# Attention heads in pairs: both heads' logit products next to each other, one output bank and one scaling per pair

## The chip, the cores and the metric

The kernel runs on one core of one Trainium2 chip. The metric is the device time of one execution in microseconds (us), as the median of several runs.

## What is computed

Two transformer blocks in sequence on 256 tokens with 2048 features, all float32. The part that the change touches is the attention of the first block: 16 "forgetting" heads (kind f, causal, with a decay added to the logits) and 16 "dilated" heads (kind d, three dilated windows merged by counting how often each key is seen), each 64 wide:

```python
proj = rms_norm(h, gain) @ w_in                       # fq fk fv fg dq dk dv
# f: p = softmax(q k^T / 8 + (c_q - c_k), causal);  o = p v
# d: q, k with rotary positions; three windows (128,1) (512,4) (2048,16);
#    o = sum over windows of softmax(lse) * softmax(q k^T / 8 in the window) v
mixed = concat(rms_norm(fox_o), rms_norm(dil_o))      # 2 x 1024 columns
h = h + mixed @ w_out
h = h + peer(rms_norm(h))                             # 16384 experts, top 16 of 8 heads
```

The second block (convolution, recurrence, gates) comes behind it and is not touched.

## The kernel before

**Weights.** All large products take their weights in units of 128x1024 floats, 512 KB each. For each unit u, SyncE loads `raw` (ring of 4), ScalarE rounds it to `whi` (`split`, line 1360), VectorE makes the rest `wlo` (`split`, line 760), and TensorE adds three products, high x high, high x low and low x high, in a PSUM bank (`group_f`, `group_t`). ScalarE and VectorE prepare unit u+3 in their step u. So ScalarE's `split(u + 3)` waits for TensorE to end unit u, and TensorE needs its result three units later.

**Units and ticks.** TensorE calls `tick(u)` behind unit u, and VectorE and ScalarE have a `step(u)` for it. Units 57 to 64 are the last dilated key projection (`dk` 1; 12 products of 512 columns per unit), units 65 to 96 are the forgetting heads' query and key projections `fq`/`fk` 0 to 7, two units each with 24 products of 256 columns per unit. The table `HEAD_START` (lines 109 to 112) hangs the 32 heads on these units, and `head_steps` spreads each over its phases:

- A: TensorE makes the logits, 64 rows deep (a head's q and k lie on rows 0 to 63 or 64 to 127 of `dqT`, `dkT`, `fqT`, `fkT`): query half 0 by 128 keys, query half 1 by 256 keys (lines 480, 481). VectorE adds the mask (for an f head made on the spot in `MB`, lines 812, 813) and takes the row's extreme (line 819), ScalarE makes the exponentials in `EB`.
- B, of d heads alone: VectorE multiplies by the counts and sums (line 824), and takes the reciprocal.
- C: TensorE turns the three 128x128 blocks round (line 490), ScalarE copies them to `PB` (line 1407).
- D: TensorE multiplies `PB` with `VV` (line 500), VectorE scales the two 64-wide results from the bank to `TM` (line 837).

A d head takes four ticks, an f head three (A, C, D). Before, heads start one per tick. An f head starts when its `fq`/`fk` pair has been copied out of its bank. f heads 14 and 15 start at ticks 97 and 98, behind the last unit, where no projection stands beside them (lines 683 to 686); the norm of `TM` and then the output projection wait for them.

The queues run in program order. The order within a tick is that of the heads' start. Small results share banks 4 to 7 in turn (`plan.side`), and whoever fills one waits until its last content is gone (`vacant`). `EB`, `PB` and `dn` have six slots.

Of the kernel before, what the change touches and what calls it, by code (L numbers as in the profile page):

```python
# [80 lines left out]
class Plan:  # L81
# [21 lines left out]
    def group(self, name, i, key, j, banks):  # L103
# [5 lines left out]
HEAD_START = [("d", h, 57 + h) for h in range(8)]  # L109
HEAD_START += [("d", 8, 67), ("d", 9, 68), ("f", 0, 69), ("f", 1, 70), ("d", 10, 71), ("d", 11, 72), ("f", 2, 73), ("f", 3, 74),  # L110
               ("d", 12, 75), ("d", 13, 76), ("f", 4, 77), ("f", 5, 78), ("d", 14, 79), ("d", 15, 80), ("f", 6, 81), ("f", 7, 82)]
HEAD_START += [("f", 2 * i + s, 69 + 4 * i + s) for i in range(4, 8) for s in range(2)]
HEAD_TICKS = range(57, 102)
TURN_AFTER = {("dq", 1): 0, ("fq", 0): 1}


def head_steps():

    at = {t: [] for t in HEAD_TICKS}
    for q, (kind, h, t) in enumerate(HEAD_START):  # L120
        for n, phase in enumerate("ABCD" if kind == "d" else "ACD"):
            at[t + n].append((q, kind, h, phase))
    return at
# [8 lines left out]
def _build(nc, I, out, ctx):  # L132
# [147 lines left out]
    HEADS = head_steps()  # L280
    hfill = {}
    for t in HEAD_TICKS:
        if t == 67:
            turns.append([plan.side() for _ in range(4)])
        for q, kind, h, phase in HEADS[t]:
            if phase != "B":
                hfill[q, phase] = plan.side()
# [161 lines left out]
    def _(e):  # L449
# [17 lines left out]
        def head(q, kind, h, phase):  # L467
            hp = slice(64 * (h % 2), 64 * (h % 2) + 64)
            ft, i = h // 2, q % 6
            vb = (0 if kind == "f" else 1024) + h * 64  # L470
            if phase == "A":
                qs, ks = QK[kind + "qT"], QK[kind + "kT"]
                if kind == "d":
                    for fill in turns[h // 8]:
                        evacuated(fill)
                else:
                    evacuated(G["fq", ft].fills[0])
                    evacuated(G["fk", ft].fills[0])
                b = vacant(hfill[q, "A"])
                mm(b[:, 0:128], qs[hp, ft, 0:128], ks[hp, ft, 0:128], True, True)  # L480
                mm(b[:, 128:384], qs[hp, ft, 128:256], ks[hp, ft, 0:256], True, True).then_inc(s_lg, 1)
            if phase == "C":
                if kind == "d":
                    w.wait_ge(s_cn, 2 * sum(k == "d" for k, _, _ in HEAD_START[:q + 1]))
                else:
                    w.wait_ge(s_ex, 2 * q + 2)
                w.wait_ge(s_const, 32)
                b = vacant(hfill[q, "C"])
                for j in range(3):
                    tr = turn_round(b[:, j * 128:j * 128 + 128], EB[:, i, j * 128:j * 128 + 128])  # L490
                tr.then_inc(s_ht, 1)
            if phase == "D":
                evacuated(hfill[q, "C"])
# [3 lines left out]
                b = vacant(hfill[q, "D"])  # L497
                for t in range(2):
                    for kt in range(t + 1):
                        ov = mm(b[:, 64 * t:64 * t + 64], PB[:, i, (t + kt) * 128:(t + kt) * 128 + 128],  # L500
                                VV[:, kt, vb:vb + 64], kt == 0, kt == t)
                ov.then_inc(s_ov, 1)
# [93 lines left out]
        def tick(u):  # L596
            if u in HEAD_TICKS and u < G["fk", 7].end:
                for q, kind, h, phase in HEADS[u]:
                    if phase != "B":
                        head(q, kind, h, phase)  # L600
# [82 lines left out]
        for u in range(G["fk", 7].end, HEAD_TICKS.stop):  # L683
            for q, kind, h, phase in HEADS[u]:
                if phase != "B":
                    head(q, kind, h, phase)
# [59 lines left out]
    def _(e):  # L746
# [50 lines left out]
        def head(q, kind, h, phase):  # L797
            i = q % 6
            vb = (0 if kind == "f" else 1024) + h * 64
            E, d = EB[:, i, :], dn[:, i, :]  # L800
            cs = [slice(0, 128), slice(128, 384)]
            nf = sum(k == "f" for k, _, _ in HEAD_START[:q])
            nd = q - nf
            if phase == "A":
                if q >= 6:
                    w.wait_ge(s_ht, q - 5)
                    evacuated(hfill[q - 6, "D"])
                w.wait_ge(s_att, 32)
                M = MB[:, nf % 4, :]
                if kind == "f":  # L810
                    w.wait_ge(s_cb, 16)
                    tt(M[:, 0:128], mskF[:, 128:256], CB[:, h, 0:128], ALU.subtract).then_inc(s_mask, 1)
                    tt(M[:, 128:384], mskF, CB[:, h, :], ALU.subtract).then_inc(s_mask, 1)
                    w.wait_ge(s_mask, 2 * nf + 2)
                b, n = hfill[q, "A"]
                w.wait_ge(s_lg, q + 1)
                for t in range(2):
                    m_ = M[:, cs[t]] if kind == "f" else mskD if t else mskF[:, 128:256]
                    e.tensor_tensor_reduce(E[:, cs[t]], banks[b][:, cs[t]], m_, -1.0, 3.0e38,  # L819
                                           ALU.add, ALU.min, d[:, t:t + 1]).then_inc(s_free[b] if t else s_mx, 1)  # L820
            if phase == "B":
                w.wait_ge(s_ex, 2 * q + 2)
                for t in range(2):
                    e.tensor_tensor_reduce(E[:, cs[t]], E[:, cs[t]], cnt1 if t else cnt0, 1.0, 0.0,
                                           ALU.mult, ALU.add, d[:, 2 + t:3 + t]).then_inc(s_cn, 1)
                w.wait_ge(s_cn, 2 * nd + 2)
                e.reciprocal(d[:, 4:6], d[:, 2:4]).then_inc(s_rd, 1)
            if phase == "C" and kind == "f":
                w.wait_ge(s_ex, 2 * q + 2)
                e.reciprocal(d[:, 4:6], d[:, 2:4]).then_inc(s_rd, 1)  # L830
            if phase == "D":
                b, n = hfill[q, "D"]
                w.wait_ge(s_ov, q + 1)
                w.wait_ge(s_rd, q + 1)
                w.wait_ge(s_turn, 4 if q < 8 else 8)
                for t in range(2):
                    o = e.tensor_scalar(TM[:, t, vb:vb + 64], banks[b][:, 64 * t:64 * t + 64], d[:, 4 + t:5 + t], None, ALU.mult)
                o.then_inc(s_free[b], 1)
# [222 lines left out]
        def step(u):  # L1061
            if u in HEAD_TICKS and u < G["fk", 7].end:
                for q, kind, h, phase in HEADS[u]:
                    head(q, kind, h, phase)
# [77 lines left out]
        for u in range(G["fk", 7].end, HEAD_TICKS.stop):  # L1142
            for q, kind, h, phase in HEADS[u]:
                head(q, kind, h, phase)

        for fill in hfill.values():
            evacuated(fill)
        w.wait_ge(s_ov, 32)
# [193 lines left out]
    def _(e):  # L1342
# [46 lines left out]
        def head(q, kind, h, phase):  # L1389
            i = q % 6  # L1390
            E, d = EB[:, i, :], dn[:, i, :]
            cs = [slice(0, 128), slice(128, 384)]
            if phase == "A":
                w.wait_ge(s_mx, q + 1)
                evacuated(hfill[q, "A"])
                for t in range(2):
                    if kind == "f":
                        act(E[:, cs[t]], E[:, cs[t]], ACT.Exp, bias=d[:, t:t + 1], scale=-1.0,
                            accum_out=d[:, 2 + t:3 + t]).then_inc(s_ex, 1)
                    else:  # L1400
                        act(E[:, cs[t]], E[:, cs[t]], ACT.Exp, bias=d[:, t:t + 1], scale=-1.0).then_inc(s_ex, 1)
            if phase == "C":
                b, n = hfill[q, "C"]
                if q >= 6:
                    w.wait_ge(s_ov, q - 5)
                w.wait_ge(s_ht, q + 1)
                act(PB[:, i, :], banks[b][:, 0:384], ACT.Copy).then_inc(s_free[b], 1)
# [72 lines left out]
        def step(u):  # L1480
            if u in HEAD_TICKS and u < G["fk", 7].end:
                for q, kind, h, phase in HEADS[u]:
                    head(q, kind, h, phase)
# [61 lines left out]
        for u in range(G["fk", 7].end, HEAD_TICKS.stop):  # L1545
            for q, kind, h, phase in HEADS[u]:
                head(q, kind, h, phase)
        warm()

        for fill in hfill.values():  # L1550
            evacuated(fill)
        w.wait_ge(s_ov, 32)
# [203 lines left out]
```

## Time and profile before

| what | value |
|---|---|
| median of 3 runs | 3015.35 us (3012.07 to 3016.42) |
| the profiled execution's own time | 3016.64 us |
| its span, first to last instruction | 3014.9 us |
| TensorE matmul busy | 2931.1 us, 97% of the span |
| VectorE, ScalarE busy | 1816.1 us (60%), 1349.6 us (45%) |
| mean granted TensorE clock | 0.986 of full |
| the heads' stretch, tick 57 to the last head's scaling | from 185.56 us to 376.69 us |

PE is TensorE's matmuls, PEld its weight loads, DVE is VectorE, ACT ScalarE. A float32 product is made in two passes, each with a weight load: one head's phase A is 4 loads and 4 matmuls in the trace, phase D is 6, phase C is 3. A matmul's duration in a row runs until its result is out, and matmuls overlap; how fast they follow each other is read from their starts.

### The profile page before, as it was taken

How to read it: one execution, taken by the hardware profiler on the slowest of the kernel's cores; microseconds unless marked ns; L12 is line 12 of the kernel's file. 1: busy time of each engine (PE TensorE's matmuls, PEld its weight loads, DVE VectorE, ACT ScalarE, POOL GpSimd, SP SyncE). 2: the span in 40 equal slices, each digit the busy share in tenths (PEclk: the TensorE clock that was granted, in tenths of full speed). 3: DMA queues.
4: the chain of work that ended last, by engine and by line, in shares of the span. 5: the costliest groups of instructions: out<-in, count | busy, mean ns of one | idle time of the engine just before them, and what ended most of it. 6: DMA issues, size and time to landing. Idle time of an engine off the chain costs nothing. (4 is left out here: it accounts for less than half of the span.)

```text
span 3014.9 us, 47881 instructions
## 1 busy us (share of the span) xinstructions
PE 2931.1 (97%) x19478; PEld 2698.1 (89%) x19478; DVE 1816.1 (60%) x3033; ACT 1349.6 (45%) x1809; POOL 0.2 (0%) x4
## 2 busy tenths in 40 slices
PE   8999999999999999999999999997999999999988
PEld 6878878999999999998888888886989999999876
DVE  5556555477888874444555555556577765555555
ACT  4444444344444444444444444444554544444444
POOL 0000000000000000000000000000000000000000
PEclk9999999999999999999999999998999999999999
DMA  6643346455556665556666677764554455555554
GB/s 211 209 136 109 123 148 201 151 184 183 183 182 210 210 216 183 182 186 195 222 221 222 205 232 237 235 210 159 160 183 147 147 164 188 184 183 182 187 166 157
DMA packets 180091, 557.33 MB, mean 185 GB/s; under 512 B 20624, under 2 KB 51616, under 8 KB 176928
## 3 DMA queue, kind: packets, MB, share of 16 engines
q1 hardware_dynamic: 177568, 537.49, 55.0%
q10 hardware_dynamic: 2304, 16.78, 1.4%
q8 instruction: 155, 2.54, 0.3%
q14 instruction: 64, 0.52, 0.1%
HBM read 533.21 MB, written 20.99 MB: 184 GB/s over the span
## 5 line engine op out<-in xcount | busy, mean ns | idle before, releaser
L760 DVE TENSOR_TENSOR wlo<-raw,whi 128x1024 fp32r<-128x1024 f32 (+1 forms) x965 | 1180.0, 1224 | 1051.4 <-ACT whi L1352 1048.2
L1352 ACT ACTIVATE whi<-raw 128x1024 fp32r<-128x1024 f32 (+1 forms) x965 | 1017.2, 1056 | 1055.4 <-PE bank L453 1040.6
L453 PE MATMUL bank<-aH,whi 128*128 128x256 f32 (+1 forms) x3984 | 1138.7, 286 | 0.0
L453 PE MATMUL bank<-aH,wlo 128*128 128x256 f32 (+1 forms) x3984 | 1128.3, 283 | 2.0 <-DVE wlo L760 2.0
L453 PE MATMUL bank<-aL,whi 128*128 128x256 f32 (+1 forms) x3984 | 1127.1, 283 | 0.0
L453 PE MATMUL bank<-whi,aH 128*128 128x512 f32 x2624 | 859.2, 391 | 5.2 <-DVE aH L763 3.8
L453 PEld LDWEIGHTS bank<-aH,whi 128*128 128x128 f32 (+1 forms) x3984 | 762.9, 191 | 8.2 <-issue 7.6
L453 PEld LDWEIGHTS bank<-aH,wlo 128*128 128x128 f32 (+1 forms) x3984 | 762.0, 191 | 3.2 <-DVE wlo L760 2.6
L453 PEld LDWEIGHTS bank<-aL,whi 128*128 128x128 f32 (+1 forms) x3984 | 762.5, 191 | 0.5
L453 PE MATMUL bank<-wlo,aH 128*128 128x512 f32 x1600 | 625.1, 391 | 0.8 <-DVE wlo L760 0.8
L453 PEld LDWEIGHTS bank<-whi,aH 128*128 128x128 f32 x2624 | 494.6, 188 | 111.3 <-DVE aH L763 4.0
L453 PEld LDWEIGHTS bank<-wlo,aH 128*128 128x128 f32 x1600 | 301.7, 189 | 64.3 <-DVE wlo L760 2.0
L453 PE MATMUL bank<-whi,aL 128*128 128x512 f32 x576 | 225.2, 391 | 0.0
L1352 ACT ACTIVATE aH<-HB 128x256 fp32r<-128x256 f32 x128 | 53.5, 418 | 214.2 <-DVE HB L763 214.2
L1352 ACT ACTIVATE HB<-bank 128x256 f32<-128x256 f32 (+1 forms) x192 | 85.0, 443 | 123.7 <-PE bank L453 123.7
L453 PEld LDWEIGHTS bank<-whi,aL 128*128 128x128 f32 x576 | 108.7, 189 | 22.5
L763 DVE TENSOR_TENSOR aH<-HB,aH 128x256 fp32r<-128x256 f32 x128 | 54.3, 425 | 61.9 <-ACT aH L1352 61.9
L894 DVE TENSOR_SCALAR HB<-small,HB 128x128 f32<-128x128 f32 x256 | 87.4, 341 | 0.0
L453 PE MATMUL bank<-HB 128*128 128x128 f32 x576 | 77.6, 282 | 3.1 <-DVE HB L1174 3.1
L453 PEld LDWEIGHTS bank<-HB 128*128 128x128 f32 x576 | 72.6, 198 | 3.3 <-issue 3.3
L893 DVE TENSOR_SCALAR HB<-small,HB 128x128 f32<-128x128 f32 x256 | 71.8, 280 | 0.0
L1352 ACT ACTIVATE EB<-EB,dn 128x128 f32<-128x128 f32 x64 | 27.2, 448 | 76.6 <-DVE dn L819 76.5
(183 smaller groups left out, 1653.8 us busy)
## 6 DMA issues: line engine op xcount, KB each, us to landing
raw<-in_w_down SPq DMA_DIRECT2D x256, 512.0 KB, 3.6
raw<-in_w_up SPq DMA_DIRECT2D x256, 512.0 KB, 3.8
raw<-in_w_in SPq DMA_DIRECT2D x176, 512.0 KB, 3.6
raw<-in_w_out SPq DMA_DIRECT2D x32, 512.0 KB, 3.8
raw<-in_w_pq SPq DMA_DIRECT2D x32, 512.0 KB, 4.2
gate_scratch<-HB ACTq DMA_DIRECT2D x16, 1024.0 KB, 4.9
raw<-in_w_o SPq DMA_DIRECT2D x32, 512.0 KB, 4.2
raw<-in_w_pg SPq DMA_DIRECT2D x32, 512.0 KB, 4.1
```

The source lines that it names most:

```text
L453: return e.matmul(o, lhsT, rhs, start=start, stop=stop, skip_group_check=True)
L760: e.tensor_tensor(wlo[:, s, 0:n], raw[:, r, 0:n], whi[:, s, 0:n].bitcast(F32), ALU.subtract).then_inc(s_lo, 1)
L763: return e.tensor_tensor(o, a, b, op)
L893: e.tensor_scalar(AB[:, i, 0, c, :], iota, JT[:, 0, t:t + 1], None, ALU.is_equal).then_inc(s_oh, 1)
L894: e.tensor_scalar(AB[:, i, 1, c, :], iota, JT[:, 1, t:t + 1], JT[:, 2, t:t + 1], ALU.is_equal, ALU.mult).then_inc(s_oh, 1)
L1352: return e.activation(o, i, f, **k)
```

## The change

The heads are taken in pairs (2i, 2i+1). `PAIRS` starts 16 pairs where 32 heads started: d pairs at ticks 57, 59, 61, 63, 67, 71, 75, 79 and f pairs at 69, 73, 77, 81, 85, 89, 93, 97. In phase A the two heads' products alternate, head 2i on rows 0 to 63 and head 2i+1 on rows 64 to 127, into two banks. C has two banks, D writes both heads into one bank, and one VectorE operation scales 128x256 values to `TM`. The reciprocals of a pair are one operation. The ring of six slots now holds three pairs.

```diff
-HEAD_START = [("d", h, 57 + h) for h in range(8)]
...
+PAIRS = [("d", 0, 57), ("d", 1, 59), ("d", 2, 61), ("d", 3, 63), ("d", 4, 67), ("f", 0, 69), ("d", 5, 71), ("f", 1, 73),
+         ("d", 6, 75), ("f", 2, 77), ("d", 7, 79), ("f", 3, 81), ("f", 4, 85), ("f", 5, 89), ("f", 6, 93), ("f", 7, 97)]
...
-            if phase != "B":
-                hfill[q, phase] = plan.side()
+            if phase in "AC":
+                hfill[q, phase] = [plan.side(), plan.side()]
+            if phase == "D":
+                hfill[q, phase] = [plan.side()]
... TensorE
-                b = vacant(hfill[q, "A"])
-                mm(b[:, 0:128], qs[hp, ft, 0:128], ks[hp, ft, 0:128], True, True)
-                mm(b[:, 128:384], qs[hp, ft, 128:256], ks[hp, ft, 0:256], True, True).then_inc(s_lg, 1)
+                b = [vacant(fill) for fill in hfill[q, "A"]]
+                for t in range(2):
+                    for x in range(2):
+                        hp = slice(64 * x, 64 * x + 64)
+                        lg = mm(b[x][:, 128 * t:128 + 256 * t], qs[hp, pair, 128 * t:128 * t + 128], ks[hp, pair, 0:128 * t + 128], True, True)
+                        if t:
+                            lg.then_inc(s_lg, 1)
...
+                    w.wait_ge(s_ex, 4 * q + 4)
...
+                for fill in hfill[q, "C"]:
+                    evacuated(fill)
...
+                for t in range(2):
+                    for x in range(2):
+                        for kt in range(t + 1):
+                            ov = mm(b[:, 128 * t + 64 * x:128 * t + 64 * x + 64],
+                                    PB[:, 2 * (q % 3) + x, (t + kt) * 128:(t + kt) * 128 + 128],
+                                    VV[:, kt, vb + 64 * x:vb + 64 * x + 64], kt == 0, kt == t)
... VectorE
+                for x in range(2):
...
+                        w.wait_ge(s_mask, 4 * nf + 2 * x + 2)
+                    b, n = hfill[q, "A"][x]
+                    w.wait_ge(s_lg, 2 * q + x + 1)
...
-                for t in range(2):
-                    o = e.tensor_scalar(TM[:, t, vb:vb + 64], banks[b][:, 64 * t:64 * t + 64], d[:, 4 + t:5 + t], None, ALU.mult)
-                o.then_inc(s_free[b], 1)
+                tt(TM[:, :, vb:vb + 128].rearrange("p t (x c) -> p t x c", x=2),
+                   banks[b][:, 0:256].rearrange("p (t x c) -> p t x c", t=2, x=2),
+                   d2[:, :, 4:6].rearrange("p x t -> p t x").unsqueeze(3).to_broadcast([128, 2, 2, 64]), ALU.mult).then_inc(s_free[b], 1)
```

**TensorE between two units of the `dk` projection.** Before, every tick from 60 to 64 holds one head's D, the next one's C and a third one's A (`VV,PB` is D, `small,EB` is C, `dkT,dqT` is A; the first and the last row are the projection):

```order
L453 MATMUL bank<-whi,aL 128x512
L453 MATMUL bank<-VV,PB 128x64 x3
L465 MATMUL bank<-small,EB 128x128 x3
L453 MATMUL bank<-dkT,dqT 128x128
L453 MATMUL bank<-dkT,dqT 128x256
L453 MATMUL bank<-whi,aH 128x512
```

With the change an odd tick holds C of one pair and A of the next:

```order
L452 MATMUL bank<-whi,aL 128x512
L464 MATMUL bank<-small,EB 128x128 x6
L452 MATMUL bank<-dkT,dqT 128x128 x2
L452 MATMUL bank<-dkT,dqT 128x256 x2
L452 MATMUL bank<-whi,aH 128x512
```

The even ticks hold D alone, `VV,PB 128x64 x6`. The two heads' A products now stand together, once every second unit.

**TensorE behind the last unit.** Before (two single heads, 14 and 15, one D of head 13 ahead of them; the last row is the norm's transposes):

```order
L453 MATMUL bank<-aH,wlo 128x256
L453 MATMUL bank<-VV,PB 128x64 x3
L453 MATMUL bank<-fkT,fqT 128x128
L453 MATMUL bank<-fkT,fqT 128x256
L465 MATMUL bank<-small,EB 128x128 x3
L453 MATMUL bank<-fkT,fqT 128x128
L453 MATMUL bank<-fkT,fqT 128x256
L453 MATMUL bank<-VV,PB 128x64 x3
L465 MATMUL bank<-small,EB 128x128 x3
L453 MATMUL bank<-VV,PB 128x64 x3
L465 MATMUL bank<-small,VV 128x128 x32
```

With the change (one pair):

```order
L452 MATMUL bank<-aH,wlo 128x256
L452 MATMUL bank<-fkT,fqT 128x128 x2
L452 MATMUL bank<-fkT,fqT 128x256 x2
L464 MATMUL bank<-small,EB 128x128 x6
L452 MATMUL bank<-VV,PB 128x64 x6
L464 MATMUL bank<-small,VV 128x128 x32
```

The two heads go through A, C and D together, in three steps where there were four, and no D stands ahead of them.

**VectorE behind the last unit, with the change** (the second head's masks, its two sums with the logits, then the pair's reciprocal and scaling, and the norm's first square):

```order
L768 TENSOR_TENSOR MB<-attc,CB 128x128
L768 TENSOR_TENSOR MB<-attc,CB 128x256
L825 ISA EB,dn<-bank,MB 128x128
L825 ISA dn 128x1
L825 ISA EB,dn<-bank,MB 128x256
L825 ISA dn 128x1
L838 RECIPROCAL dn<-dn 128x2x2
L768 TENSOR_TENSOR TM<-bank,dn 128x2x128
L771 ISA VV,st<-TM 128x512
```

The second head's masks stand behind the first head's logits on VectorE; before they stood behind the whole of the first head's A.

## Rows read from the trace of the kernel before

**Rows 1.** The page, part 1: busy time, share of the span, instructions
```profile
PE 2931.1 (97%) x19478; PEld 2698.1 (89%) x19478; DVE 1816.1 (60%) x3033; ACT 1349.6 (45%) x1809; POOL 0.2 (0%) x4
```

**Rows 2.** Busy time by stretch: f units, bare tail; PEclk, DMA share, GB/s last
```profile
235.00:365.00 130.00, 128.23 (x989) 117.48 (x987) 72.99 (x246) 62.78 (x139) 0.00 (x0) 1.00 0.36 116
365.00:378.00 13.00, 7.28 (x26) 5.15 (x26) 4.79 (x20) 5.84 (x17) 0.00 (x0) 0.56 0.24 81
```

**Rows 3.** Timeline, PE alone, ticks 91 to 94: start us, duration us, group
```profile
345.22 0.36 PE L453 MATMUL bank<-aH,whi 128*128 128x256 f32 x1
...
348.77 0.36 PE L453 MATMUL bank<-aH,whi 128*128 128x256 f32 x1
...
352.67 0.38 PE L453 MATMUL bank<-aH,whi 128*128 128x256 f32 x1
...
355.64 0.49 PE L465 MATMUL bank<-small,EB 128*128 128x128 f32 x3
356.06 0.92 PE L453 MATMUL bank<-fkT,fqT 64*128 64x128 f32 x4
356.91 0.39 PE L453 MATMUL bank<-aH,whi 128*128 128x256 f32 x1
357.13 0.28 PE L453 MATMUL bank<-aL,whi 128*128 128x256 f32 x1
357.25 0.28 PE L453 MATMUL bank<-aH,wlo 128*128 128x256 f32 x1
```

**Rows 4.** The same A stretch, timeline cut at its third and fourth pass
```profile
356.39 0.59 PE L453 MATMUL bank<-fkT,fqT 64*128 64x256 f32 x2
...
356.61 0.38 PE L453 MATMUL bank<-fkT,fqT 64*128 64x256 f32 x1
```

**Rows 5.** Timeline, tick 69: PE's C and A, ACT's work ahead
```profile
243.29 0.49 PE L465 MATMUL bank<-small,EB 128*128 128x128 f32 x3
244.07 0.89 PE L453 MATMUL bank<-fkT,fqT 64*128 64x128 f32 x4 [0.28 <-issue]
...
242.66 1.04 ACT L1352 ACTIVATE whi<-raw 128x1024 fp32r<-128x1024 f32 x1
243.61 0.36 ACT L1352 ACTIVATE fkT<-bank 128x256 f32<-128x256 f32 x1
```

**Rows 6.** Timeline, PE at tick 66: D, C, second half of the turning
```profile
227.94 0.78 PE L453 MATMUL bank<-VV,PB 128*128 128x64 f32 x6
...
229.27 0.55 PE L465 MATMUL bank<-small,EB 128*128 128x128 f32 x3 [0.55 <-DVE dn L824]
...
231.09 1.06 PE L465 MATMUL bank<-small,TM 128*128 128x128 f32 x8 [0.40 <-DVE TM L837]
```

**Rows 7.** Timeline, DVE and ACT around tick 68: wlo, B of a d head, exponentials
```profile
239.25 1.23 DVE L760 TENSOR_TENSOR wlo<-raw,whi 128x1024 fp32r<-128x1024 f32 x1 [1.95 <-ACT whi L1352]
240.39 0.28 DVE L824 CUSTOM_DVE_ANT_0 EB<-EB,attc 128x128 f32<-128x128 f32 x1
...
241.06 0.17 DVE L827 RECIPROCAL dn<-dn 128x2 f32<-128x2 f32 x1
...
241.95 0.80 ACT L1352 ACTIVATE EB<-EB,dn 128x128 f32<-128x128 f32 x2 [2.80 <-DVE dn L819]
```

**Rows 8.** Timeline of all engines behind the last unit, heads 14 and 15
```profile
365.40 0.89 PE L453 MATMUL bank<-fkT,fqT 64*128 64x128 f32 x4 [0.91 <-issue]
366.27 0.62 DVE L763 TENSOR_TENSOR MB<-attc,CB 128x128 f32<-128x128 f32 x2
366.92 0.29 DVE L819 CUSTOM_DVE_ANT_0 EB<-bank,MB 128x128 f32<-128x128 f32 x1
...
368.46 0.18 ACT L1352 ACTIVATION_READ_ACCUMULATOR EB<-EB,dn 128x1 f32 x1
...
368.70 0.90 PE L465 MATMUL bank<-small,EB 128*128 128x128 f32 x3 [2.42 <-ACT EB L1352]
...
369.70 0.49 ACT L1352 ACTIVATE PB<-bank 128x384 f32<-128x384 f32 x1 [1.05 <-PE bank L465]
...
374.64 1.54 PE L453 MATMUL bank<-VV,PB 128*128 128x64 f32 x6 [0.64 <-ACT PB L1352]
376.22 0.47 DVE L837 TENSOR_SCALAR TM<-bank,dn 128x64 f32<-128x64 f32 x2 [2.97 <-PE bank L453]
```

More of the change, by code:

```diff
@@ L465, in turn_round, with heads @@
             return e.transpose(o, src, ident)
[L467 to L470, printed above, removed]
+        def heads(q, kind, pair, phase):
             if phase == "A":
@@ L597, in tick @@
             if u in HEAD_TICKS and u < G["fk", 7].end:
-                for q, kind, h, phase in HEADS[u]:
+                for q, kind, pair, phase in HEADS[u]:
                     if phase != "B":
-                        head(q, kind, h, phase)
+                        heads(q, kind, pair, phase)
             if DOWN0 <= u < DOWN0 + ROUTE:
@@ L683, in _ @@
         for u in range(G["fk", 7].end, HEAD_TICKS.stop):
-            for q, kind, h, phase in HEADS[u]:
+            for q, kind, pair, phase in HEADS[u]:
                 if phase != "B":
-                    head(q, kind, h, phase)
+                    heads(q, kind, pair, phase)
         norm_turn(1, VV)
@@ L795, in tails, with heads @@
                     hook(kp)
[L797 to L800, printed above, removed]
+        def heads(q, kind, pair, phase):
+            vb = (0 if kind == "f" else 1024) + pair * 128
+            e0 = 2 * (q % 3)
+            d2 = dn[:, e0:e0 + 2, :]
             cs = [slice(0, 128), slice(128, 384)]
-            nf = sum(k == "f" for k, _, _ in HEAD_START[:q])
+            nf = sum(k == "f" for k, _, _ in PAIRS[:q])
@@ L1062, in step @@
             if u in HEAD_TICKS and u < G["fk", 7].end:
-                for q, kind, h, phase in HEADS[u]:
-                    head(q, kind, h, phase)
+                for q, kind, pair, phase in HEADS[u]:
+                    heads(q, kind, pair, phase)
             if u == G["dq", 0].first + 1:
@@ L1142, in _ @@
         for u in range(G["fk", 7].end, HEAD_TICKS.stop):
-            for q, kind, h, phase in HEADS[u]:
-                head(q, kind, h, phase)
-        for fill in hfill.values():
+            for q, kind, pair, phase in HEADS[u]:
+                heads(q, kind, pair, phase)
+        for fill in [x for y in hfill.values() for x in y]:
             evacuated(fill)
-        w.wait_ge(s_ov, 32)
+        w.wait_ge(s_ov, 16)
         for c in range(1, 8, 2):
@@ L1481, in step @@
             if u in HEAD_TICKS and u < G["fk", 7].end:
-                for q, kind, h, phase in HEADS[u]:
-                    head(q, kind, h, phase)
+                for q, kind, pair, phase in HEADS[u]:
+                    heads(q, kind, pair, phase)
             if DOWN0 <= u < DOWN0 + ROUTE:
```

134 lines of the change are left out of this document (63 added, 71 removed).

## The prediction

> **What bounds the kernel now.** I read the page first: TensorE's matmuls are busy for 97% of the span, VectorE 60%, ScalarE 45% [rows 1]. Then the busy time by stretch, for the place that the change touches: among the `fq`/`fk` units TensorE is busy for 128.2 of 130 us at full clock while VectorE works 73.0 us and ScalarE 62.8 us, and the DMA share is 0.36; behind the last unit TensorE works 7.3 of 13 us at a mean granted clock of 0.56 [rows 2]. So there are two kinds of place. Among the units only time on TensorE's own queue counts, its waits included. Behind the last unit it is a chain through all three engines. The timeline then prices both, and 0.2% of the kernel, 6 us, is about what a measurement can tell from no change.
>
> **Pace of TensorE.** Projection products of 256 columns follow each other every 0.12 us (357.13 to 357.25), so a bare unit of 24 takes 2.88 us [rows 3]. From one unit's first product to the next one's it is 3.55 us with a D between (345.22 to 348.77), 3.90 us with an A (348.77 to 352.67), 4.24 us with a C and an A (352.67 to 356.91) [rows 3]. So D costs 0.67, A 1.02 and C 0.34 us. What is in A? Its 256-column pass takes 0.22 us (356.39 to 356.61) [rows 4], a 128-column pass half of it, so its four passes are 0.66 us. The other 0.36 us belong to the change of form, from 128-row products to 64-row ones and back. Half of it is seen at the way out: the last pass is followed after 0.30 us, not 0.22 (356.61 to 356.91), and the first projection product after 0.22, not 0.12 (356.91 to 357.13) [rows 3, 4]. The other half is at the way in.
>
> **The change, part by part.**
>
> *Logit products side by side.* The same passes, in half as many stretches. Of 32 stretches 30 stood among units, and 15 stand there now, so 15 ways in and out go: 15 x 0.36 = 5.4 us. What the two halves of the rows do to each other no row shows, since no two A stretches touch before. Bounds: at worst each of the three steps from one half to the other inside a pair costs what the change of form costs, 3 x 0.36 = 1.08 us, 16.2 us over 15 pairs (that is a rival below). At best passes of different halves overlap. The order is head 0 twice, head 1 twice, for 128 columns and then for 256; with starts in that order the second pass of one head can cover the first of the other, and a pair's 1.32 us would shrink by 0.43, which is 6.4 us over 15. But each pass needs a weight load of 128 columns, and if loads come one after the other at the 0.11 us of the short passes, the short ones cannot overlap at all and only one 0.22 us pass is covered: 0.2 us per pair, 3.1 us. I take half of that smaller gain, 1.6 us, because the rows nearest to it, the single stretches, show passes strictly one after the other.
>
> The Trainium skill ("TensorEngine Tiling (Array Packing)", Key Properties) says that changing the tiling mode drains TensorE and changing only the tile does not, so by it the steps inside a pair would be free; no row here shows that half of the rule.
>
> *The new ticks.* C and D have the passes they had. A pair's D is 12 passes in one stretch; what its ends cost is within hundredths of a us, taken as nothing.
>
> *Waits of TensorE that go.* At tick 69 A starts 0.78 us behind C's start, where 0.42 is the normal step (355.64 to 356.06) [rows 3, 5]. ScalarE copies `fkT` out until 243.97, and that copy is late because the exponentials of the head of tick 68 and a split of 1.04 us stand ahead of it [rows 5]. This recurs at ticks 73, 77 and 81. With the change ticks 68, 72, 76 and 80 have no A, and the copy is done within some 1.5 us of the unit's end, a whole unit before it is needed: 4 x 0.35 = 1.4 us. At tick 66 C starts 1.33 us behind D, 0.7 more than D's 6 passes take, waiting for a B that VectorE runs behind the rotary work; then the turning waits 0.40 us for the scaling of a head [rows 6]. With the change the last B of the `dk` part is in tick 64, ahead of the rotary work, and the scaling finds VectorE free: 1.1 us.
>
> *One D that loses its cover.* Behind the last unit TensorE waits 0.91 us for the copy of `fkT` before A [rows 8], and head 13's D lies ahead of that wait, hidden. With the change the D of f pair 6 is in tick 95 and nothing stands there: 0.6 us given back.
>
> *VectorE.* The scaling is 1 operation for a pair where 4 stood, and a reciprocal goes. It works 73 of 130 us there [rows 2], so among units this is worth nothing. New on it: a pair's A holds the masks and sums of two heads in a row, and ScalarE's two sets of exponentials come ahead of the split for the unit three further on. That delays `whi` by 0.7 to 0.9 us where two whole units lie in between. No load is moved, and the ring of four raw buffers is ahead at a DMA share of 0.36.
>
> *New lateness, C against the softmax.* Count from the end of A's stretch on TensorE. An f pair: first sums done at 0.4 (they start when that head's own passes are done, ahead of the other's last two), second masks 0.62, second sums 0.65 and the exponentials 1.07 behind them (sums from 366.92, exponentials to 368.64 [rows 8]), so 2.8 us. The next C comes after a unit, 2.97 us, in the last four f pairs, and after a unit and a D in the others. It is met by 0.1 us. A d pair: two sums end at 1.1, two exponentials of 0.8, split 1.04, `wlo` 1.23, then B of both heads at 0.67 each [rows 7] end near 5.6; C comes after two units, 5.8 us. Met by 0.2 us. I cost both at nothing.
>
> *Behind the last unit.* Before, the scaling ends at 376.69 [rows 8]. With the pair, counting on the same clock: first sums at 366.92 as before (VectorE sets that, not TensorE), second sums end 0.65 + 0.62 + 0.65 later at 368.84, exponentials at 369.91, C 369.97, its second half 0.65 later (three passes at half clock), `PB` of the second head from 371.62 to 372.11, D with 12 passes where 6 took 1.58 us from 374.64 to 376.22, so 1.58 + 6 x 0.22 = 2.9 us, and one scaling of 0.42 us: 375.5. That is 1.2 us earlier. The norm and the output projection follow as they did.
>
> **Sum.** 5.4 + 1.6 + 1.4 + 1.1 - 0.6 + 1.2 = 10.1 us less than the profiled execution's 3016.6. That execution is 1.3 us above the median of the runs, so I forecast 3015.35 - 10.1, about **3005 us**. The granted clock adds noise that no term carries: the bare tail runs at half clock in stretches that end where they end, and starting the next work 9 us earlier against them can win or lose 2 us.
>
> **The rivals.**
>
> 1. *Full overlap of the halves.* The loads too would run side by side, and the gain on top of 8.5 us is 6.4 instead of 1.6: 15 us, 3000.4 us. For it: the halves share no row and no bank. Against it: every pass in the rows of a stretch waits for its load. The Trainium skill ("TensorE: Matmul & The Clock Gate", Part 3) says that matmuls in different row groups start some 4 ns apart, and that loads overlap matmuls of another group; taken alone for this order that is this rival, and no row here shows it. Chance 0.14.
>
> 2. *The step between halves costs as much as the change of form* (the other side). The pair's three inner steps, 1.08 us, are more than the 0.36 it saves, so 15 x 0.72 = 10.8 us are lost on TensorE, another 2 us behind the last unit, where the clock is half; against it stand the 3.1 us of waits and tail, and the time is 3015.35 + 9.7 = 3025 us. It decides from 0.6 us per pair of inner steps on. For it: the change of form is dear, and nothing shows that it is not the step of rows that is paid. Against it: no wait is needed between halves that share nothing. Chance 0.07.
>
> 3. *The softmax of a pair misses C.* The margins above are 0.1 and 0.2 us. If every one of 15 pairs made TensorE wait 0.4 us, 6 us come back, and 4 us remain: 3011 us, within 0.2%. For it: all latencies grow by one head's work. Against it: 4 of the f pairs have a D ahead of C, which gives 1.2 us more. Chance 0.17.
>
> 4. *Given back later*: the earlier finish meets an unlucky run of half-clock stretches, here and in the later stages. Then 3 to 5 us stay: 3011 us. Chance 0.07.
>
> **How the numbers follow.** The forecast (8 to 13 us gained) has 0.55. Faster by over 0.2% takes the forecast, rival 1 and a part of rivals 3 and 4: 0.77. Within 0.2%: the rest of those two, 0.15. Slower: rival 2 and a little for what I don't see, 0.08. The range leaves out rival 2 and the tails of the others: it reaches from full overlap, 3000 us, to rivals 3 and 4, 3012 us.
>
> **What the profile after would show.** 16 A stretches of 8 passes. If I am right, an A tick of one pair costs 1.5 to 1.7 us over the bare unit, not 2.04; if rival 1 is, below 1.3; if rival 2 is, above 2.4. C follows A at ticks 69, 73, 77, 81 in 0.34 us per head, and `fkT` is no longer what A waits for. Rival 3 shows as PE idle ahead of `small,EB`, released by ScalarE's `EB` or VectorE's `dn`. Tick 66 has no gap. Behind the last unit it should be 10.1 us from A's start to the scaling's end, not 11.3. Wrong above all would be a stretch elsewhere that changes, since nothing behind the first block's heads is touched.

## The result and the profile after

| what | before | with the change |
|---|---|---|
| median | 3015.35 us (5 runs) | 2998.84 us (5 runs, 2992.67 to 2999.56) |
| ratio | | 0.9943, 95% interval 0.9929 to 0.9958 |
| span of the profiled execution | 3014.9 us | 2990.9 us |

It is 16.5 us faster by the medians, 0.57% (0.42 to 0.71%) by the ratio. The direction is as forecast, the size is not: 10.1 us were predicted, and 2998.8 lies 1.2 us under the range.

The page after, part 1, to be held against [rows 1]:

```profile
PE 2908.7 (97%) x19478; PEld 2684.3 (90%) x19478; DVE 1806.9 (60%) x2969; ACT 1348.0 (45%) x1809; POOL 0.2 (0%) x4
```

TensorE has the same 19478 matmuls and is busy for 22.4 us less, so time was saved while it works, not only in its waits (a part of it is the granted clock, see below). Busy time by stretch, first the ticks 69 to 94, then the bare tail, as in [rows 2]:

```profile
235.00:345.00 110.00, 109.78 (x920) 104.14 (x919) 62.94 (x191) 57.41 (x130) 0.00 (x0) 1.00 0.41 130
347.50:359.00 11.50, 5.26 (x26) 4.33 (x26) 4.19 (x15) 5.76 (x14) 0.00 (x0) 0.63 0.26 85
```

Among the units nothing but TensorE is short: it is busy for all but 0.2 of 110 us. The table cuts both traces at the same five points of the program. The times are differences of starts in the trace.

| from ... to ... | before | after | gain |
|---|---|---|---|
| first A ... first C | 10.60 us | 8.01 us | 2.6 |
| first C ... last product of unit 96 | 167.43 | 153.05 | 14.4 |
| that product ... last scaling to `TM` | 13.11 | 11.75 | 1.4 |
| last scaling ... output projection's first product | 11.42 | 10.81 | 0.6 |
| together | 202.56 | 183.62 | 18.9 |

The 14.4 us are the step to explain. Timeline of an A stretch of a pair, PE alone, the same place in a unit as [rows 3]:

```profile
305.38 0.28 PE L452 MATMUL bank<-aL,whi 128*128 128x256 f32 x1
305.50 0.28 PE L452 MATMUL bank<-aH,wlo 128*128 128x256 f32 x1
305.71 0.93 PE L452 MATMUL bank<-fkT,fqT 64*128 64x128 f32 x8
306.57 0.38 PE L452 MATMUL bank<-aH,whi 128*128 128x256 f32 x1
306.79 0.28 PE L452 MATMUL bank<-aL,whi 128*128 128x256 f32 x1
```

The eight passes of a pair take 0.86 us until the next projection product (305.71 to 306.57). The four passes of one head took 0.85 (356.06 to 356.91 [rows 3]). Two heads cost what one did. Cut the same timeline at 305.80 us and the view shows how:

```profile
305.71 0.38 PE L452 MATMUL bank<-fkT,fqT 64*128 64x128 f32 x2
```

Two passes have started, and together they last 0.38 us, hardly more than one. The trace's own starts of the eight are 305.713 and 305.720, then 305.927 and 305.933, 306.038 and 306.045, 306.257 and 306.264: the halves of the rows run as a pair of passes 7 ns apart, weight loads included.

The price of a pair is 1.07 us from the last product before it to the first one behind it, and 0.10 for the slower step after that (306.57 to 306.79, where 0.12 is normal), less the 0.12 of a normal step: 1.05 us. Two single heads cost 2.04 by the prediction's count, and 2.08 when they are counted at the same places as the pair. The period of the f pairs decides between the two: from A at tick 89 to A at tick 93 before takes 15.53 us (336.29 to 351.82) and after 14.82 (320.55 to 335.37), of which 0.29 are a new wait of C (below), so a pair saves 1.00 us, and 2.04 is the better count. Between the first C and the last unit's end lie 28 single A before and 14 pairs after, so 28 x 1.02 - 14 x 1.05 = 13.9 us. The waits that went give 2.5 us, the D without cover takes 0.6 and new waits of C 1.4: 14.4, which is the whole of that stretch.

The waits are gone as forecast. Timeline of PE at ticks 66 and 69, to be held against [rows 6] and [rows 5]:

```profile
223.47 1.45 PE L452 MATMUL bank<-VV,PB 128*128 128x64 f32 x12
224.75 1.92 PE L464 MATMUL bank<-small,TM 128*128 128x128 f32 x16
...
236.24 0.87 PE L464 MATMUL bank<-small,EB 128*128 128x128 f32 x6
237.04 0.93 PE L452 MATMUL bank<-fkT,fqT 64*128 64x128 f32 x8
```

At tick 66 the turning follows 1.28 us behind the start of D's twelve passes. At tick 69 A starts 0.80 us behind C, which is now six passes. No row has a bracket for a wait.

Two small waits are new, and the PE view does not mark them either, because they hide in the overlap of pipelined matmuls. PE at tick 90, and what ScalarE does there:

```profile
309.42 0.28 PE L452 MATMUL bank<-aH,wlo 128*128 128x256 f32 x1
309.78 0.87 PE L464 MATMUL bank<-small,EB 128*128 128x128 f32 x6
310.41 0.36 PE L452 MATMUL bank<-aH,whi 128*128 128x256 f32 x1
...
309.14 0.49 ACT L1360 ACTIVATE EB<-EB,dn 128x256 f32<-128x256 f32 x1
309.54 0.19 ACT L1360 ACTIVATION_READ_ACCUMULATOR EB<-EB,dn 128x1 f32 x1
```

C starts 0.36 us behind the last product, where 0.12 is normal, and right behind the second head's last exponential (309.54 + 0.19 = 309.73). With the step behind it that is 0.29 us, at ticks 86, 90 and 94; four d pairs lose 0.12 each.

Behind the last unit, all engines, to be held against [rows 8]:

```profile
348.46 0.36 ACT L1360 ACTIVATE fkT<-bank 128x256 f32<-128x256 f32 x1
...
348.92 0.93 PE L452 MATMUL bank<-fkT,fqT 64*128 64x128 f32 x8 [1.52 <-issue]
...
353.44 1.54 PE L464 MATMUL bank<-small,EB 128*128 128x128 f32 x6 [3.59 <-ACT EB L1360]
354.44 1.07 ACT L1360 ACTIVATE PB<-bank 128x384 f32<-128x384 f32 x2 [1.05 <-PE bank L464]
...
355.61 2.79 PE L452 MATMUL bank<-VV,PB 128*128 128x64 f32 x12 [0.63 <-ACT PB L1360]
358.44 0.42 DVE L768 TENSOR_TENSOR TM<-bank,dn 128x256 f32<-128x256 f32 x1 [4.84 <-PE bank L452]
```

From A's start to the scaling's end it is 9.95 us (348.92 to 358.87). The chain is one of waits: C waits for both heads' exponentials, D for both copies, the scaling for all twelve passes.

**The granted clock.** The profiled executions differ by 24 us, the medians by 16.5. Behind the output projection's first product no instruction was changed, and yet that rest took 2626.7 us before and 2621.2 after. TensorE's clock was at 1.2 GHz (granted clock 0.5) for 47.8 us of it before and for 34.1 us after, not counting what lies behind TensorE's last matmul. In nine of the eleven profiled executions of this study the rest less half of its half-clock time lies between 2602.8 and 2604.3 us; the other two have 2604.8 (e7_table_tail) and 2601.7 (e8_table_again). So the half-clock time, which runs from 34.1 to 47.8 us, is worth up to 6.8 us from one execution to the next, and what it leaves unexplained up to 3 us. One such place, 193.4 us behind that first product, by stretch, in the profile after and in a second execution of the same program (columns as in [rows 2]):

```profile
563.10:569.90 6.80, 6.11 (x55) 6.14 (x55) 4.37 (x8) 0.00 (x0) 0.00 (x0) 1.00 0.31 96
```

```profile
562.80:569.60 6.80, 5.56 (x26) 5.59 (x27) 2.34 (x5) 0.00 (x0) 0.00 (x0) 0.50 0.37 125
```

Same program, same work, 55 matmuls in 6.8 us in one and 26 in the other. Ahead of it TensorE was idle for most of the time in both, busy for 0.72 of 3.1 us and for 0.88 of 2.8 us. So below I compare the stretch from the first A to the output projection's first product, which does not depend on the rest, and use the medians as the check. What this comparison does not see is time that an edit adds ahead of the first A (see e9_table_tail_exp).

### The profile page after: what moved, and what is told of

Same layout as the page of the kernel before. It is cut to its first block and busy times, and to the rows that moved or that the text cites. A ratio compares the mean times of both kernels' runs of the same rounds, so it can differ in the third digit from the quotient of the medians.

```text
span 2990.9 us, 47745 instructions
## 1 busy us (share of the span) xinstructions
PE 2908.7 (97%) x19478; PEld 2684.3 (90%) x19478; DVE 1806.9 (60%) x2969; ACT 1348.0 (45%) x1809; POOL 0.2 (0%) x4
## 5 line engine op out<-in xcount | busy, mean ns | idle before, releaser
L452 PEld LDWEIGHTS bank<-whi,aL 128*128 128x128 f32 x576 | 108.5, 188 | 22.4
L768 DVE TENSOR_TENSOR HB<-HB,aL 128x256 f32<-128x256 f32 x126 | 52.8, 419 | 0.0
```

What stands on the lines that cost most here:

```text
L452: return e.matmul(o, lhsT, rhs, start=start, stop=stop, skip_group_check=True)
L768: return e.tensor_tensor(o, a, b, op)
```

## The experiments

The theory after the result is **lockstep** (OVERLAP in the expectations): passes of the two halves run side by side, so a pair costs one head. The rivals: it needs the alternating order; it is the single change of form that pays, not the overlap (MERGE); or the gain is in the joint bank and scaling.

Stretches in us, from the trace of each kernel's profiled execution. "Units" is from the first C to the last product of unit 96, "copy" from there to the last pair's A (before: to head 14's), "tail" from A to the end of the last scaling, "norm" from there to the output projection.

| kernel | first A to C | units | copy | tail | norm | together |
|---|---|---|---|---|---|---|
| before | 10.60 | 167.43 | 1.81 | 11.30 | 11.42 | 202.56 |
| after | 8.01 | 153.05 | 1.80 | 9.95 | 10.81 | 183.62 |
| e1_again | 8.07 | 152.98 | 1.80 | 9.95 | 10.83 | 183.64 |
| e2_same_half | 8.67 | 160.69 | 1.81 | 9.94 | 10.82 | 191.92 |
| e3_head_after_head | 7.89 | 153.10 | 1.80 | 9.94 | 10.99 | 183.72 |
| e4_table_alone | 8.05 | 151.72 | 1.85 | 8.35 | 10.63 | 180.60 |
| e5_turn_per_head | 9.48 | 151.60 | 1.80 | 9.30 | 10.81 | 183.00 |
| e6_output_per_head | 8.03 | 153.06 | 1.85 | 9.35 | 10.63 | 182.92 |
| e7_table_tail | 7.33 | 152.18 | 0.84 | 8.38 | 11.32 | 180.05 |
| e8_table_again | 9.48 | 151.71 | 1.85 | 8.35 | 10.63 | 182.02 |
| e9_table_tail_exp | 6.48 | 151.81 | 0.84 | 8.23 | 10.30 | 177.66 |

### e1_again: the change once more

No edit.

> The changed kernel once more, on the chip of the next three, so that they can be held against it. Theory OVERLAP: the two heads' passes run at the same time on the two halves of the rows, so a pair's phase A (8 passes) takes 0.86 us from its first product to the next projection product, as one head's did. Theory MERGE: the gain is the saved changes of form and waits, the rest was a lucky granted clock. Both expect a ratio to the kernel before of 0.994 to 0.996 here; OVERLAP expects 0.86 us per stretch again, and 183 to 185 us from the first A to the first output projection product (before 202.6).

Measured: 3000.17 us (2994.41 to 3000.52), 3013.45 before on that chip, ratio 0.995 (0.9936 to 0.9963). The stretch repeats to 0.02 us. Its rest has the 47.8 us of half clock that before has, and with those equal the spans differ by 3014.9 - 2997.1 = 17.8 us: that is the change with most of the clock's luck taken out (the first pair still has 1.5 us of it, see below).

### e2_same_half: both heads on rows 0 to 63

```diff
-                        hp = slice(64 * x, 64 * x + 64)
+                        hp = slice(0, 64)
```

> Both heads of a pair read q and k of the even head, rows 0 to 63, so head 2i's logits are made twice and head 2i+1's not at all; passes, banks, order and all other work stay. OVERLAP: the stretch grows by one head's four passes, 0.66 us, to 1.5 us; 15 x 0.66 = 9.9 us among units and some 0.9 us behind them (the first head's logits come while VectorE is still busy, the second's too): 10 us slower than the changed kernel, ratio to before 0.997 to 0.998. MERGE: no difference from the changed kernel.

Measured: 3003.67 us (3002.78 to 3004.81), ratio 0.9967 (0.9955 to 0.9979). Its A stretch, timeline of PE:

```profile
312.35 0.28 PE L452 MATMUL bank<-aH,wlo 128*128 128x256 f32 x1
312.56 1.57 PE L452 MATMUL bank<-fkT,fqT 64*128 64x128 f32 x8
314.07 0.39 PE L452 MATMUL bank<-aH,whi 128*128 128x256 f32 x1
```

The stretch is 1.51 us instead of 0.86, so the overlap is worth 0.65 us per pair. That is the 0.66 us of one head's passes, all of it. Over 15 pairs it is 9.8 us. The units grew by 7.6 us: 14 x 0.65 = 9.1, less the 1.4 us of C's waits, which vanish since a longer A gives the softmax more time. What remains against before, 202.56 - 191.92 = 10.6 us, is what the change gives without overlap, 1.5 us of it by the clock in the first pair (below). The rival that puts all of the gain on the change of form falls. The odd heads' logits are not computed here, so this kernel is of use for its time alone. By the medians it is 3.5 us slower than e1_again, not the 10 that were expected: the stretch is 8.3 us longer (the waits of C went, and the tail did not grow by the expected 0.9), and its profiled execution has 6.8 us less half clock in the rest (41.0 against 47.8), which is worth 3.4. So the 0.65 us per pair are read from the trace, and the medians give only their direction.

### e3_head_after_head: the order of the passes

```diff
-                for t in range(2):
-                    for x in range(2):
+                for x in range(2):
+                    for t in range(2):
```

> The four products of a pair in the order head 0 (128, 256 keys), head 1 (128, 256 keys), not alternating. OVERLAP with starts in program order: only the last pass of head 0 and the first of head 1 can overlap, so the stretch is 1.2 to 1.4 us, 5 to 8 us slower than the changed kernel. OVERLAP with a queue for each half: stretch 0.86 us, time as the changed kernel within 1 us. MERGE: as the changed kernel.

Measured: 2997.79 us (2996.75 to 2999.6), ratio 0.9946 (0.9932 to 0.9959). TensorE is given both products of head 2i and then both of head 2i+1. Its timeline, and the same cut at 305.40 us:

```profile
305.25 0.93 PE L452 MATMUL bank<-fkT,fqT 64*128 64x128 f32 x8
306.11 0.38 PE L452 MATMUL bank<-aH,whi 128*128 128x256 f32 x1
```

```profile
305.25 0.39 PE L452 MATMUL bank<-fkT,fqT 64*128 64x128 f32 x2
```

It still takes 0.86 us, and the two short passes at its start (305.245 and 305.258 in the trace, 13 ns apart) are followed by two more at 305.46. The two wide passes of one head start with the two of the other (305.570 and 305.583). If starts kept the program's order, head 2i would have run its four passes first. The trace does not name the head of a pass; it is read from the columns, two short passes and two wide ones per head. So the order plays no part here: a pass waits for its own half's passes and not for the up to four that were issued ahead of it on the other half.

### e4_table_alone: the kernel before with the new starts

```diff
-HEAD_START = [("d", h, 57 + h) for h in range(8)]
...
+PAIRS = [("d", 0, 57), ("d", 1, 59), ("d", 2, 61), ("d", 3, 63), ("d", 4, 67), ("f", 0, 69), ("d", 5, 71), ("f", 1, 73),
+         ("d", 6, 75), ("f", 2, 77), ("d", 7, 79), ("f", 3, 81), ("f", 4, 85), ("f", 5, 89), ("f", 6, 93), ("f", 7, 97)]
+HEAD_START = [(kind, 2 * pair + x, t) for kind, pair, t in PAIRS for x in range(2)]
```

Everything else stays per head: its own C wait, D bank and scaling.

> The kernel before with only its table of starts changed: heads 2i and 2i+1 start at the same tick, each with its own bank, its own D and two scalings of its own, products head after head. If the place of the heads is all that matters and each half has a queue: within 1 us of the changed kernel (the single scaling is worth 0.5 us behind the last unit). If starts go in program order: 5 to 8 us slower than the changed kernel. MERGE: as the changed kernel.

Measured: 2991.75 us (2990.43 to 2994.84), ratio 0.993 (0.9917 to 0.9944). Since TensorE's queue holds the two heads' A next to each other here too, the table alone brings the whole overlap: the eight passes of a pair take 0.86 us again, read as above from PE's timeline:

```profile
304.95 0.93 PE L452 MATMUL bank<-fkT,fqT 64*128 64x128 f32 x8
305.82 0.38 PE L452 MATMUL bank<-aH,whi 128*128 128x256 f32 x1
```

The stretch is 3.0 us shorter than with the full change, where within 1 us was expected. Its tail, all engines:

```profile
350.62 0.90 PE L464 MATMUL bank<-small,EB 128*128 128x128 f32 x3 [2.33 <-ACT EB L1351]
...
351.84 0.91 PE L464 MATMUL bank<-small,EB 128*128 128x128 f32 x3 [0.31 <-ACT EB L1351]
352.54 2.66 PE L452 MATMUL bank<-VV,PB 128*128 128x64 f32 x12
...
353.96 0.47 DVE L836 TENSOR_SCALAR TM<-bank,dn 128x64 f32<-128x64 f32 x2 [1.98 <-PE bank L452]
...
355.24 0.48 DVE L836 TENSOR_SCALAR TM<-bank,dn 128x64 f32<-128x64 f32 x2 [0.81 <-PE bank L452]
```

The first head's C, D and scaling each run while the second head is one step behind. The joint waits of the change take that overlap away, 8.35 us against 9.95.

### e5_turn_per_head and e6_output_per_head: which joint step costs the 3 us

e5 is the change with one wait for C per head:

```diff
-                if kind == "d":
-                    w.wait_ge(s_cn, 4 * sum(k == "d" for k, _, _ in PAIRS[:q + 1]))
-                else:
-                    w.wait_ge(s_ex, 4 * q + 4)
...
+                    if kind == "d":
+                        w.wait_ge(s_cn, 4 * sum(k == "d" for k, _, _ in PAIRS[:q + 1]) - 2 + 2 * x)
+                    else:
+                        w.wait_ge(s_ex, 4 * q + 2 * x + 2)
```

> The changed kernel, but each head's transposes (phase C) wait for that head's softmax and not for the pair's. Read from the first A to the first output projection product (183.6 us in the changed kernel, 180.6 with the table alone). Theory TURN: the pair's common wait ahead of C is what the changed kernel loses against the table alone: C's late starts of 0.12 us at d pairs and 0.24 us at f pairs go, and behind the last unit the first head's C and copy lie under the second head's exponentials, 0.65 us; 181.5 to 182.5 us in all. Theory OUTPUT: the common D and single scaling is what costs: this run changes nothing, 183.6 us.

e6 is the change with an output bank and a scaling per head:

```diff
-                hfill[q, phase] = [plan.side()]
+                hfill[q, phase] = [plan.side(), plan.side()]
...
+                for x in range(2):
+                    evacuated(hfill[q, "C"][x])
+                    b = vacant(hfill[q, "D"][x])
...
```

> The changed kernel, but phase D with a bank, a semaphore step and two scalings for each head, as before the change; A and C stay paired. TURN: only what lies behind the last unit changes, where the first head's scaling lies under the second's D and the second's D waits alone for its copy: 0.3 to 0.9 us; 182.7 to 183.3 us. OUTPUT: most of the 3 us come back, below 181.5 us. Among units both expect no gain from or loss to the three more operations on VectorE, which waits there anyway.

Measured, one run each: e5 2993.44 us, e6 2994.7 us; the verdict rests on the stretches. In e5 the units lose 1.45 us and the tail 0.65. C of tick 90 again follows after a normal 0.12 us:

```profile
309.90 0.28 PE L452 MATMUL bank<-aH,wlo 128*128 128x256 f32 x1
310.02 0.82 PE L464 MATMUL bank<-small,EB 128*128 128x128 f32 x6
310.60 0.36 PE L452 MATMUL bank<-aH,whi 128*128 128x256 f32 x1
```

Its first A to C is longer (9.48) because that execution spent 6.5 us there at half clock and the one of after 3.4; e4_table_alone and e8_table_again, one program, differ in the same way (8.05 and 9.48). In e6 the units do not move (153.06): one scaling instead of four saves nothing where TensorE is the bound. Tail and norm lose 0.6 and 0.2 us, since D of the first head no longer waits for the second copy: it starts 1.54 us behind C, where 2.17 passed with the change. Together e5 and e6 give 1.45 + 0.65 + 0.6 + 0.2 = 2.9 us, and e4_table_alone gains 3.0. The joint steps are settled for this kernel: they cost 3 us of the stretch and bring nothing.

### e7_table_tail: e4 with the masks a tick early and the last copy ahead of a split

```diff
+    for q, (kind, h, t) in enumerate(HEAD_START):
+        if kind == "f":
+            at[t - 1].append((q, kind, h, "M"))
...
-            split(u + NSPL)
+            if u != G["fk", 7].end - 1:
+                split(u + NSPL)
...
+            if u == G["fk", 7].end:
+                split(u - 1 + NSPL)
```

> The table alone, with the f heads' masks made one tick early on VectorE, and, behind the last unit, ScalarE's copy of fkT and both heads' phase A put ahead of the split for the unit three further on. What should go is the chain behind the last unit: the copy is 1.04 us earlier, and neither the split of 1.22 us nor 0.62 us of masks per head stands between the logits and their sums: 10.2 us from the last projection product to the last scaling should become 8 to 8.7 us. Units as in the table alone, 159.8 us. First A to first output product 178.8 us; ratio to before 0.991 to 0.993.

### e8_table_again: e4 once more, on the same chip

> The table alone once more, beside e7 on the same chip: 180.6 us from the first A to the first output product again, and a ratio to before of 0.992 to 0.994. If its lead over the changed kernel was only clock luck, 0.995. Once the first output projection product has started, every kernel so far took 2603.6 us (2602.9 to 2604.1) plus half of the time at half clock in the profile up to the last stretch; this should hold again.

Measured: e7 2992.9 us (2989.93 to 2994.2), ratio 0.9929 (0.9916 to 0.9943); e8 2993.72 us (2993.44 to 2995.16), ratio 0.9935 (0.9921 to 0.9949). The copy of `fkT` came 1.0 us sooner, but the tail stayed at 8.38. ACT and PE there:

```profile
345.64 0.38 ACT L1360 ACTIVATE fkT<-bank 128x256 f32<-128x256 f32 x1 [3.09 <-PE bank L455]
346.16 0.93 PE L455 MATMUL bank<-fkT,fqT 64*128 64x128 f32 x8 [0.56 <-ACT fkT L1360]
...
349.74 1.04 ACT L1360 ACTIVATE whi<-raw 128x1024 fp32r<-128x1024 f32 x1
350.68 0.84 ACT L1360 ACTIVATE PB<-bank 128x384 f32<-128x384 f32 x2
```

The split that I had moved out of the copy's way stands ahead of the `PB` copies now, 1.04 us of it. No run separates it from the masks; the tail as a whole gained nothing. From the last projection product to the last scaling it is 9.2 us, where 8 to 8.7 were expected. In e8_table_again the stretch is 182.02 us, not the 180.6 expected: 1.43 us more in the first A to C, at 6.5 us of half clock instead of 3.4, and 0.01 elsewhere. Its rest is under the expected 2602.9 to 2604.1 us (2601.7).

### e9_table_tail_exp: that split further back, and the table load ahead

e7 with the split behind tick 98 on both engines, and one small exponential ahead of the heads, so that ScalarE's table is there:

```diff
+        act(st[:, 31:32], cols[:, 0:1], ACT.Exp).then_inc(s_warm, 1)
...
-            if u == G["fk", 7].end:
-                split(u - 1 + NSPL)
+            if u == G["fk", 7].end + 1:
+                split(u - 2 + NSPL)
```

> e7_table_tail with two more edits: the split that was postponed stands behind the last copies to PB (both engines), not ahead of them, and ScalarE makes one exponential of one column ahead of the dk units, so that the 1.28 us load of its table is out of the first pair's chain. Theory (each of the two is a link of a chain that TensorE waits for): from the last pair's A to the last scaling 8.38 in e7_table_tail becomes 7.4 (the 1.04 us split gone from between exponentials and PB), the copy of fkT still starts 0.84 us behind the last projection product; from the first A to the first C 7.3 us or 8.0 become 6.7 or less at full clock; from the first A to the first product of the output projection 178.5 to 179.5 us where e7_table_tail took 180.05, ratio to the kernel before 0.992. Rival (what ends these stretches is TensorE's own half clock and not the engines' chain): both stretches stay within 0.3 us of e7_table_tail, ratio 0.993. The rest of the kernel, behind the output projection's first product, stays at 2603 to 2605 us plus half of its half-clock time.

Measured: 2993.9 us (2993.15 to 2995.49), ratio 0.9936 (0.9923 to 0.995). The stretch is the shortest of all, 177.66 us, 6.0 under the change. The first A to C is 6.48 us, 0.85 less than in e7_table_tail, neither with any half clock: the table load was a link of the first pair's chain, as this kernel expected. In e3_head_after_head, where TensorE was never at half clock there, the load and the wait read:

```profile
187.30 1.28 ACT L1360 ACT_TABLE_LOAD   x1 [6.67 <-DVE dn L825]
...
193.54 0.88 PE L464 MATMUL bank<-small,EB 128*128 128x128 f32 x6 [1.29 <-DVE dn L832]
```

But the load was moved and not saved. It now stands ahead of three splits, and TensorE waits for `wlo` (ACT, then PE):

```profile
118.02 1.28 ACT L1360 ACT_TABLE_LOAD   x1
119.31 0.21 ACT L1360 ACTIVATE st<-cols 128x1 f32<-128x1 f32 x1
119.42 2.98 ACT L1360 ACTIVATE whi<-raw 128x1024 fp32r<-128x1024 f32 x3
...
121.85 0.50 PE L455 MATMUL bank<-wlo,aH 128*128 128x512 f32 x1 [0.37 <-DVE wlo L762]
...
136.32 0.50 PE L455 MATMUL bank<-wlo,aH 128*128 128x512 f32 x1 [0.58 <-DVE wlo L762]
```

The first A starts at 187.06 us, where every other kernel has it between 185.56 and 186.05 and e7_table_tail at 185.81. That is 1.25 us lost ahead of the stretch for 0.85 gained in it.

The tail missed its 7.4: it took 8.23. The split's other half, on VectorE, is in front of the scaling:

```profile
352.43 1.23 DVE L762 TENSOR_TENSOR wlo<-raw,whi 128x1024 fp32r<-128x1024 f32 x1 [2.37 <-ACT whi L1360]
353.57 0.85 DVE L842 TENSOR_SCALAR TM<-bank,dn 128x64 f32<-128x64 f32 x4
```

And the whole kernel is no faster than e4 or e7, though its stretch is 2.4 us shorter than e7's. 1.25 us of the 2.4 are paid ahead of the first A. The other 1.1 us are less than the clock moves: its profiled execution has 47.8 us of half clock in the rest, e7's 41.0, which is worth 3.4 us. Whether the clock takes this gain back every time, or did so in these five runs, stays open.

The kernels that keep the new starts and drop the joint steps (e4, e7, e9) lie between 0.9929 and 0.9936 of the kernel before, the change itself at 0.9943 and 0.995. All these intervals overlap, so the times alone don't rank them; their medians, 2991.75 to 2993.9 us against 2998.84 and 3000.17, and the stretches, which repeat to hundredths of a us at the same clock (e9's with the 1.25 us ahead of it counted), both put the three ahead.

## Why the prediction was right in direction and too small

- **The step that failed is "I take half of that smaller gain, 1.6 us, because the rows nearest to it, the single stretches, show passes strictly one after the other".** The rows were read rightly, but they were all rows of one half. A pass that follows another on its own half says nothing of a pass on the other. Measured: 0.65 us per pair, 9.8 us over 15, six times the term and more than both bounds I set as the best case (3.1 and 6.4 us). Both bounds assumed one queue, in the program's order, as the description of the kernel says of all queues. e2_same_half priced the term and e3_head_after_head showed that on TensorE this does not hold between the two halves of the rows.
- Rival 1 (full overlap, 15 us) named the mechanism and had its size too small for the same reason. The rule that I set beside it, the Trainium skill's "TensorE: Matmul & The Clock Gate", Part 3, agrees in that passes of different row groups start some nanoseconds apart (7 ns here); its words that matmuls start and end strictly in order do not agree with e3_head_after_head, where the measurement decides.
- Rival 2 falls: no step between the halves costs anything. This is the half of the rule in the Trainium skill's "TensorEngine Tiling (Array Packing)", Key Properties, that no row of before showed. The trace agrees: 0.86 us for eight passes, where one head's four take 0.85, leaves no room for a drain between them.
- The change of form, 0.36 us per stretch, was right. With the passes of one head at 0.66 us, a pair costs 1.05 us, and 1.02 were to be expected. e2_same_half gives it by itself: a pair there costs 1.05 + 0.65 = 1.70 us where two single heads cost 2.04, so one change of form less is worth 0.34.
- The waits at ticks 69, 73, 77 and 81 (1.4 us) and at tick 66 (1.1 us) went. The D without cover (-0.6) came. The balance of the units closes with them to some 0.1 us.
- "I cost both at nothing", C against the softmax: the margins of 0.1 and 0.2 us were wrong by 0.3. The waits are 0.29 us in three f pairs and 0.12 in four d pairs, 1.4 us; e5_turn_per_head takes them away. It is rival 3 with a quarter of its price. The prediction counts four f pairs with only a unit ahead of C; the one at tick 97 stands behind the units, so there are three.
- The first pair is the fifteenth of the stretches, so its share stands in the terms. With nearly the same half-clock time in both (6.8 and 6.5 us), it gives 10.60 - 9.48 = 1.1 us, about what a pair saves. The other 1.5 us in the profiles of before and after is the clock, for which I had no term.
- Behind the last unit I forecast 10.1 us from A's start to the scaling's end, and it is 9.95. The 1.2 us were 1.35. That this is worse than two heads one step apart on the same ticks (8.35 in e4_table_alone) I did not see: I took the joint D and scaling as given and weighed them against the four steps of before alone.
- VectorE's four scalings against one: nothing, as forecast.

With the overlap at its measured size and the C waits in, the sum is 5.4 + 9.8 + 1.4 + 1.1 - 0.6 + 1.4 - 1.4 = 17.1 us. With the first pair's 1.5 us of clock and the 0.6 us of the norm, for which I had no term and have no cause, it is 19.2, where the trace has 18.9 up to the output projection. The medians give 16.5 and, for e1_again, 13.3 us. So the measured 16.5 us agree with the mended sum, but 13.3 shows how loosely the medians hold it.

## What to carry to other kernels

Matmuls that are 64 rows deep should stand next to each other in TensorE's queue with their operands on different halves of the rows: the second one was then free here, in either order of the two heads' products (128 and 256 columns), and one change of form serves both. Bring work together in the queue of the engine that is the bound, but keep the waits, banks and final operations per item: a joint wait turns two chains one step apart into a single longer one. When a gain is read from one stretch, look at what the edit adds ahead of it. When a bound is taken from the nearest row, ask whether that row could have shown the effect at all.

## What was not expected of the hardware

- The two halves of TensorE's rows take their passes side by side, weight loads too, 7 ns apart (13 ns with head after head), and with head after head not in the order in which they were issued. Eight passes in 0.86 us, against 1.51 us on one half.
- Half-clock time behind the same idle time comes and goes in the same program: 34.1 us in one execution of the change and 47.8 in the next. The 6.8 us that this is worth are more than the difference between any two of the kernels e4 to e9, so a gain of a few us is better read from the stretch in which it arises.
